# Input transposes of a projection pass: from DMA to TensorE, with the scale and shift applied on the way out

## The reference, cut to what matters

```python
mod = silu(c) @ ada_w + ada_b                       # shift, scale, gate
h   = rms_norm(x, g_pre) * (1 + scale) + shift
u, q, k, v, z = split(h @ w_in)                     # 1024 each, z 2048
y_pool = multiscale_pool(u, pool_w, pool_scale)     # centred means of 2, 4, 8, 16 rows, minus the row
y_ret  = bidir_retention(rope(q), rope(k), v)       # forward and backward chunk scans, per-head norm
out = (concat(y_pool, y_ret) * silu(z)) @ w_out
y   = x + gate * rms_norm(out, g_post)
```

## Time and profile before

| | |
|---|---|
| median of the timed runs | 3350.31 us (3 runs, 3343.3 to 3356.82) |
| the profiled execution's own time | 3349.93 us |
| its span on the slowest core (6) | 3348.4 us |
| spans of the other cores | 3319.5 (core 1) to 3335.5 us (core 3); core 0 3327.2 us |
| granted TensorE clock, mean of a core | 0.976 (core 6) to 0.983 |
| TensorE busy | 3059.1 us (91%) |
| VectorE busy | 2503.0 us (75%) |
| ScalarE busy | 1259.8 us (38%) |
| GpSimd busy | 1233.1 us (37%) |

### The profile page before, as it was taken

How to read it: one execution, slowest core, us unless ns; L and a number is a source line. 1 busy time by engine, 2 the same in 40 slices (tenths; PEclk the granted TensorE clock), 3 DMA queues, 4 the chain that set the end, 5 groups by cost and what they waited for, 6 DMA issues and landing times.

```text
span 3348.4 us, 59437 instructions; the slowest of 8 cores (3319.5 to 3348.4 us)
## 1 busy us (share of the span) xinstructions
PE 3059.1 (91%) x17521; PEld 1551.3 (46%) x17824; DVE 2503.0 (75%) x4781; ACT 1259.8 (38%) x2162; POOL 1233.1 (37%) x1193
## 2 busy tenths in 40 slices
PE   1787778888899999999999999999999999999996
PEld 0343334433345555555555555555555555555553
DVE  1677877757687778877877877887877787787784
ACT  2587555655543223222322323222322222222321
POOL 1233323323333434434444434343433443443433
PEclk9899899999999999999999999999999999999998
DMA  9999999899965555555555555555555555555552
GB/s 185 206 252 243 234 226 242 238 219 241 239 214 127 130 135 140 140 136 138 132 138 137 142 133 141 138 130 137 143 134 139 140 128 140 132 145 130 140 131 73
DMA packets 727915, 542.97 MB, mean 162 GB/s; under 512 B 536112, under 2 KB 592432, under 8 KB 727600
## 3 DMA queue, kind: packets, MB, share of 16 engines
q1 hardware_dynamic: 676848, 453.15, 55.3%
q10 hardware_dynamic: 27648, 62.93, 7.3%
q0 software_dynamic: 23104, 23.07, 5.1%
HBM read 275.28 MB, written 158.86 MB: 130 GB/s over the span
## 4 chain that ended last, share of the span: by engine, by line
PE 70%; DMA 12%; ACT 5%; issue 5%; DVE 4%; POOL 2%; SPq 1%; another core or an unknown queue 1%; ACTq 1%; DVEq 0%; POOLq 0%
PE psum L772 42%; PE psum L1098 20%; PE psum L1027 4%; DMA t_hTg_105<-t_xn_102 3%; DMA t_hTg_107<-t_xn_102 2%; DMA t_hTg_106<-t_xn_102 2%; DMA t_hTg_104<-t_xn_102 1%; DMA ada_sb<-ada_w 1%; SPq L186 1%; POOL t_o_155 L1048 1%; PE psum L995 1%; ACT t_xn_102 L791 1%; PE psum L1008 1%; PE psum L1078 1%; PE psum L1079 1%
## 5 line engine op out<-in xcount | busy, mean ns | idle before, releaser
L1098 PE MATMUL psum<-t_wout,t_yT_158 128*128 128x512 bf16 x3036 | 679.9, 380 | 19.8 <-DMA t_yT_158<-t_yb_157 16.8
L1098 PEld LDWEIGHTS psum<-t_wout,t_yT_158 128*128 128x128 bf16 x3072 | 300.9, 98 | 383.3 <-issue 24.7
L772 PE MATMUL psum<-t_wqz,t_hT_125 128*128 128x512 bf16 x1503 | 344.6, 379 | 1.7
L772 PE MATMUL psum<-t_wqz,t_hT_126 128*128 128x512 bf16 x1473 | 339.0, 379 | 3.3
L772 PE MATMUL psum<-t_wqz,t_hT_127 128*128 128x512 bf16 x1475 | 334.0, 379 | 3.7 <-DVE t_fin_159 L1108 0.4
L957 POOL TENSOR_TENSOR t_kf_150<-t_krB_144,t_kdf 128x1024 bf16<-128x1024 bf16 x94 | 190.6, 2028 | 344.8 <-PE psum L1008 331.8
L998 DVE TENSOR_TENSOR t_scm_151<-psum,t_dtot 128x512 bf16<-128x512 f32 x192 | 125.5, 681 | 256.2 <-PE psum L995 247.6
L1101 ACT ACTIVATE t_fin_159<-psum 128x512 f32<-128x512 f32 x192 | 114.7, 597 | 537.2 <-PE psum L1098 534.1
L1110 POOL TENSOR_TENSOR t_xr_160<-t_xr_160,t_fin_159 128x1024 f32<-128x1024 f32 x96 | 235.7, 2455 | 168.6 <-DVE t_fin_159 L1108 168.6
L772 PEld LDWEIGHTS psum<-t_wqz,t_hT_127 128*128 128x128 bf16 x1536 | 148.8, 98 | 173.5 <-issue 0.5
L772 PEld LDWEIGHTS psum<-t_wqz,t_hT_125 128*128 128x128 bf16 x1536 | 149.0, 98 | 167.3
(11 more groups left out here) (228 smaller groups left out, 6151.0 us busy)
## 6 DMA issues: line engine op xcount, KB each, us to landing
t_xr_160<-x SPq DMA_DIRECT2D x96, 512.0 KB, 3.7
y<-t_xr_160 SPq DMA_DIRECT2D x96, 512.0 KB, 2.7
t_xin_101<-x ACTq DMA_DIRECT2D x48, 512.0 KB, 7.2
t_xin_100<-x ACTq DMA_DIRECT2D x48, 512.0 KB, 8.2
t_krB_144<-krscr SPq DMA_DIRECT2D x96, 256.0 KB, 2.8
vscr<-t_vA_118 SPq DMA_DIRECT2D x48, 256.0 KB, 7.0
krscr<-t_krA_116 SPq DMA_DIRECT2D x48, 256.0 KB, 6.5
vscr<-t_vA_119 SPq DMA_DIRECT2D x48, 256.0 KB, 6.8
```

The lines of the kernel that those rows point to most:

```text
L772: last = e.matmul(bank.ap(), hts(dc), W_[:, dc, col:col + 512], start=(dc == 0), stop=(dc == 7))
L1098: last = e.matmul(pb.ap(), yT[0][:, ec, :], wout[:, ec, sl], start=(ec == 0), stop=(ec == 15))
```

## The change

The DMA transposes of pass A's front go. For each group TensorE now transposes `xn` against an identity matrix (`ident`, made once), 16 blocks of 128x128 in two operations of eight, each operation into one PSUM bank seen as bf16. The scale and shift, until now in place in `hTg`, reads the bank and writes `hTg`: the four feature blocks of the first bank on ScalarE, those of the second on VectorE. `xin` and `ssq` get three buffers (NX), used in turn, `xn` one for each chunk of a group, and `hTg` three (NH), so the front is called one group ahead. The planner learns a cost for a transpose. Apart from that the row loads of `gate_tables` and `pool_tables` (and the loads of pool_w beside them) now wait for the last TensorE operation listed before them, as the weight loads do.

```diff
@@ -60,6 +60,9 @@
 def _est_cost(eng, calls):
     t = 0.0
     for name, a, k in calls:
+        if name == "transpose":
+            t += 0.003 + 0.000417 * 128
+            continue
         if name == "matmul":
             rhs = a[2] if len(a) > 2 else k["rhs"]
             t += 0.003 + 0.000417 * max(_free(rhs), 64)
@@ -320,7 +323,8 @@
 
 GRP = 4
 FG = 2
-NH = 4
+NH = 3
+NX = 3
 NBANKS = 8
 WARM = False
 WARM_GAP = 0.5
@@ -388,6 +392,7 @@
     aft = P([128, 8, 128], BF16, "aft")
     abt = P([128, 8, 128], BF16, "abt")
     bands = P([128, 16, 128], BF16, "bands")
+    ident = P([128, 128], BF16, "ident")
     kdf = P([128, 8], F32, "kdf")
     kdb = P([128, 8], F32, "kdb")
     gcf = P([128, 8], F32, "gcf")
@@ -514,6 +519,8 @@
     ac(lambda e: e.activation(out=scT[:, :, :], in_=cT[:, :, :], func=AF.Silu), [bf("cT")], [sc_b])
 
     dv(lambda e: e.tensor_single_scalar(out=identf[:, :], in_=diff[:, :], scalar=0.0, op=ALU.is_equal), ["diff"], ["identf"])
+    id_b = bf("ident")
+    dv(lambda e: e.tensor_copy(out=ident[:, :], in_=identf[:, :]), ["identf"], [id_b])
     dv(lambda e: e.tensor_single_scalar(out=mge[:, :], in_=diff[:, :], scalar=0.0, op=ALU.is_ge), ["diff"], ["mge"])
     dv(lambda e: e.tensor_single_scalar(out=mlt[:, :], in_=diff[:, :], scalar=0.0, op=ALU.is_lt), ["diff"], ["mlt"])
     dv(lambda e: e.tensor_scalar_max(out=rpos[:, :], in0=diff[:, :], scalar1=0.0), ["diff"], ["rpos"])
@@ -635,9 +642,10 @@
     wout_v = w_out.ap().rearrange("(ec p) n -> p ec n", p=128)
 
     def gate_tables():
-        dma("sp", gpostb[:, :], norm_post.ap().partition_broadcast(128).rearrange("p o n -> p (o n)"), w=[bf("gpostb")])
+        after = [sch.last["pe"]]
+        dma("sp", gpostb[:, :], norm_post.ap().partition_broadcast(128).rearrange("p o n -> p (o n)"), w=[bf("gpostb")], after=after)
         for s in range(nseq):
-            dma("sp", ggt[s][:, :], ada_bg.ap().partition_broadcast(128).rearrange("p o n -> p (o n)"), w=[gg_b[s]])
+            dma("sp", ggt[s][:, :], ada_bg.ap().partition_broadcast(128).rearrange("p o n -> p (o n)"), w=[gg_b[s]], after=after)
             for half in range(2):
                 pg = Bank()
 
@@ -671,10 +679,11 @@
         return paced(go)
 
     def pool_tables():
-        dma("sp", psc_row[:, :], pool_scale.ap().partition_broadcast(128).rearrange("p o n -> p (o n)"), w=[pr_b])
+        after = [sch.last["pe"]]
+        dma("sp", psc_row[:, :], pool_scale.ap().partition_broadcast(128).rearrange("p o n -> p (o n)"), w=[pr_b], after=after)
         pool_v = pool_w.ap().rearrange("g (cc p) d -> p (g cc) d", p=128)
         for hf in range(2):
-            dma("sp", pst[:, :, :], pool_v[:, hf * 4:(hf + 1) * 4, :], w=[ps_b])
+            dma("sp", pst[:, :, :], pool_v[:, hf * 4:(hf + 1) * 4, :], w=[ps_b], after=after)
             dv(lambda e, hf=hf: e.tensor_tensor(out=poolw[:, hf * 4:(hf + 1) * 4, :].rearrange("p (g c) d -> p g c d", g=2),
                                                 in0=pst[:, :, :].rearrange("p (g c) d -> p g c d", g=2),
                                                 in1=psc_row[:, hf * 512:(hf + 1) * 512].rearrange("p (g d) -> p g d", g=2).unsqueeze(2).to_broadcast([128, 2, 2, 256]),
@@ -721,10 +730,10 @@
         return ring(A, *a, log=a_bufs, **k)
 
     a_bufs.append((arena, wv_hi, wk_b + wv_b))
-    xin, xin_b = aring(2, [128, 1024], F32, "xin")
+    xin, xin_b = aring(NX, [128, 1024], F32, "xin")
     xn, xn_b = aring(2, [128, 1024], BF16, "xn")
-    hTg, hTg_b = aring(NH, [128, FG, 8, 128], BF16, "hTg", nb=FG + 8)
-    ssq, ssq_b = aring(2, [128, 4], F32, "ssq")
+    hTg, hTg_b = aring(NH, [128, FG, 8, 128], BF16, "hTg", nb=8)
+    ssq, ssq_b = aring(NX, [128, 4], F32, "ssq")
     rtA, rtA_b = aring(2, [128, 256], F32, "rtA")
     t1A, t1A_b = aring(2, [128, 512], F32, "t1A")
     t2A, t2A_b = aring(2, [128, 512], F32, "t2A")
@@ -775,32 +784,47 @@
 
     na = [0]
 
+    nx = [0]
+
     def a_front(s, g):
         gi = na[0] % NH
         na[0] += 1
         hb = hTg_b[gi]
-        Sched.inherit(hb[:FG], hb[FG:])
         for ci in range(FG - 1, -1, -1):
             c = g * FG + ci
-            sl = (nseq * 1000 - c) % 2
+            sl = nx[0] % NX
+            nx[0] += 1
             dma("act", xin[sl][:, :], xs[s].ap()[c * 128:(c + 1) * 128, :], w=xin_b[sl])
-            op("act", lambda e, sl=sl: e.activation(out=xn[sl][:, :], in_=xin[sl][:, :], func=AF.Square, accum_out=ssq[sl][:, 0:1]),
-               r=xin_b[sl], w=ssq_b[sl] + xn_b[sl])
+            op("act", lambda e, sl=sl, ci=ci: e.activation(out=xn[ci][:, :], in_=xin[sl][:, :], func=AF.Square, accum_out=ssq[sl][:, 0:1]),
+               r=xin_b[sl], w=ssq_b[sl] + xn_b[ci])
             op("pool", lambda e, sl=sl: e.tensor_scalar_add(out=ssq[sl][:, 1:2], in0=ssq[sl][:, 0:1], scalar1=float(D) * EPS), r=ssq_b[sl], w=ssq_b[sl])
             op("pool", lambda e, sl=sl: e.tensor_tensor(out=ssq[sl][:, 2:3], in0=ssq[sl][:, 1:2], in1=mhalf[:, 0:1], op=ALU.pow), r=ssq_b[sl] + [mh_b], w=ssq_b[sl])
-            op("act", lambda e, sl=sl: e.activation(out=xn[sl][:, :], in_=xin[sl][:, :], func=AF.Copy, scale=ssq[sl][:, 2:3]),
-               r=xin_b[sl] + ssq_b[sl], w=xn_b[sl])
-            dma_t("sp", hTg[gi][:, ci, :, :], xn[sl][:, :], r=xn_b[sl], w=[hb[ci]], key=hb[ci])
-        for dc in range(8):
-            v_ = hTg[gi][:, :, dc, :]
-            if dc % 2 == 0:
-                op("dve", lambda e, v_=v_, dc=dc: e.tensor_scalar(out=v_, in0=v_, scalar1=gprime[:, dc, s:s + 1], scalar2=shiftT[:, dc, s:s + 1],
-                                                                  op0=ALU.mult, op1=ALU.add), r=hb[:FG] + [gp_b], w=[hb[FG + dc]])
-            else:
-                op("act", lambda e, v_=v_, dc=dc: e.activation(out=v_, in_=v_, func=AF.Identity, scale=gprime[:, dc, s:s + 1], bias=shiftT[:, dc, s:s + 1]),
-                   r=hb[:FG] + [gp_b], w=[hb[FG + dc]])
+            op("act", lambda e, sl=sl, ci=ci: e.activation(out=xn[ci][:, :], in_=xin[sl][:, :], func=AF.Copy, scale=ssq[sl][:, 2:3]),
+               r=xin_b[sl] + ssq_b[sl], w=xn_b[ci])
+        for hf in range(2):
+            pt = Bank()
+            ptv = lambda pt=pt: pt.ap().bitcast(BF16).rearrange("p (dc t) -> p dc t", dc=4)
+
+            def tr(e, hf=hf, ptv=ptv):
+                last = None
+                for ci in range(FG):
+                    for d4 in range(4):
+                        dc = hf * 4 + d4
+                        last = e.transpose(ptv()[:, d4, ci * 128:(ci + 1) * 128], xn[ci][:, dc * 128:(dc + 1) * 128], ident[:, :])
+                return last
+            op("pe", tr, r=[x for b_ in xn_b for x in b_] + [id_b], w=[pt.b])
+            for d4 in range(4):
+                dc = hf * 4 + d4
+                dst = hTg[gi][:, :, dc, :]
+                src = lambda ptv=ptv, d4=d4: ptv()[:, d4, :].rearrange("p (c t) -> p c t", c=FG)
+                if hf == 1:
+                    op("dve", lambda e, dst=dst, src=src, dc=dc: e.tensor_scalar(out=dst, in0=src(), scalar1=gprime[:, dc, s:s + 1], scalar2=shiftT[:, dc, s:s + 1],
+                                                                                op0=ALU.mult, op1=ALU.add), r=[pt.b, gp_b], w=[hb[dc]])
+                else:
+                    op("act", lambda e, dst=dst, src=src, dc=dc: e.activation(out=dst, in_=src(), func=AF.Identity, scale=gprime[:, dc, s:s + 1],
+                                                                             bias=shiftT[:, dc, s:s + 1]), r=[pt.b, gp_b], w=[hb[dc]])
         dma("sp", rows("h", s, g * FG, FG).rearrange("(c p) n -> p c n", p=128), hTg[gi][:, :, :, :].rearrange("p c a t -> p c (a t)"),
-            r=hb[FG:], w=[scr_b[("h", s, g * FG + ci)] for ci in range(FG)], key=hb[FG])
+            r=hb, w=[scr_b[("h", s, g * FG + ci)] for ci in range(FG)], key=hb[0])
         return gi
 
     nA = [0]
@@ -811,7 +835,7 @@
         r3 = nA[0] % 2
         nA[0] += 1
         ci = c % FG
-        hb = hTg_b[gi][FG:]
+        hb = hTg_b[gi]
         hts = lambda dc: hTg[gi][:, ci, dc, :]
         dma("act", rtA[r3][:, :], ropescr.ap()[c * 128:(c + 1) * 128, :], r=[rsb[c // GRP]], w=rtA_b[r3])
         pv = [Bank(), Bank()]
```

## The result

The changed kernel takes 3250.81 us (median; lowest 3245.67) beside 3351.98 us for the kernel before: a ratio of 0.9696, with an interval of 0.9668 to 0.9724. The forecast was 3260 us. Some executions of any of these kernels are disturbed (the cores of one die run longer at a lower granted clock); ratios leave these out, and where an experiment had too few others, its undisturbed cores are compared. The profiled execution took 3250.5 us; its slowest core is core 2 with a span of 3249.0 us.

What follows compares the result with a forecast made beforehand. Pass A was taken as bound by the arrival of transposed input. Stretch savings of 84.5 us, plus 12 for the prologue, less 6 for row loads, gave 90.5 off 3350.3: 3260 us; range 3200 to 3340.

Steps and rivals of the forecast that it cites:

- So pass A is bound by the arrival of transposed input: Pass A, the first 996 us: TensorE waits for DMA transposes into hTg, which hold 27.6% of the chain of waits.
- The stores behind the transposes: SP's queue in pass A: stores of kr, v and b go out sooner once 96 transposes leave; credited nothing.
- The DMA rival: Pass A: DMA engines stay the bound after the transposes leave, 3293 to 3317, say 3305 us; chance 0.16.
- The rate in the tail: After pass A's inputs: 196 GB/s at DMA share 0.61, some 320 at 1, held against DMA staying the bound.
- Transposes on TensorE, 0.45 us a chunk: Pass A: eight 128x128 transposes a chunk at 0.056 us each, so TensorE needs 7.80 us a chunk.
- the fourth case: Pass A: TensorE stands at its transposes, 2.8 us at each of 47 groups, 132 us, time 3392; chance 0.09.
- VectorE 0.38 for 0.28 us an evacuation: Scale and shift reading PSUM: 0.38 us each on VectorE, 0.2 us a chunk more; ScalarE no change.
- Prologue -12 us: Before the first chunk: 2.1 MB less to load at 175 GB/s, 12 us earlier; bounds 0 and 15.
- 100 to 200 us, -13 and +6 for the rows: 9.7 chunks: TensorE's 82.6 us of work at 95% busy takes 87, saving 13; waits for tied row loads cost 6.
- 200 to 300 us, ScalarE full, -5.5: 10.4 chunks: ScalarE stays at 89.8 us with rope and decay tables; at 95% busy 94.5, saving 5.5.
- 300 to 450 us, -19: 13.7 chunks: VectorE, with band tables, has 124.5 us of work; at 95% busy 131, saving 19.
- 450 to 950 us, TensorE at 95%, -47: 54.3 chunks: TensorE has 431 us of work; at 95% busy 453, saving 47.

Runs made afterwards that it cites:

- the first experiment: Changed kernel with 96 idle DMA transposes put back, one a chunk into an unread spare tile, and two xin buffers: 0.996 of before.
- the control: Changed kernel with two xin buffers in place of three, without any idle transposes: 0.9713 of before.
- the idle copies of 256 B: Changed kernel, two xin buffers, plus an idle plain 256 KB copy a chunk in 1024 runs of 256 bytes: no ratio, lowest time 3244.41 us.
- the tables spread: Changed kernel with set-up tables spread over more chunks and loads for pass B moved later: 0.9628 of before, about 3226 us.
- the early rows: Changed kernel with set-up work spread, plus gate row loads tied to chunk 4 and pool row loads to chunk 55: 0.9636 of before.
- four transposes of 128x128 a chunk: Changed kernel, two xin buffers, plus four idle 128x128 DMA transposes a chunk: 0.9848 of before.

## Why the prediction came out right, and what was wrong in it

The time was right, and the signature it named came: pass B at 896 us for 905 and 2352 us long, clock 0.98 to 0.99, DMA share under 1, transposes 56 ns apart. One sign did not come: 200 to 300 us was to be hardly shorter. By its steps:

- *"So pass A is bound by the arrival of transposed input"*: this step failed. The chain showed where waits ended, and those were the transposes; but with the wait gone and the load left, they end at the stores, and the time is within 0.4% of that before. What held pass A was what the transposes do to the other transfers: 2.9 us a chunk of all the DMA engines, and SP's queue held. The share of 1.03 to 1.12 in the earlier trace rows said the first.
- *The stores behind the transposes, "for which I credit nothing, as TensorE waits for none of them directly"*: this is where the load was left out. VectorE and ScalarE wait for them, 76 us in 400 in the first experiment, since kr and v have two buffers each; GpSimd's scaled k comes after kr, and TensorE stands 24 us behind that (4 in the control). The number held all the same, because the change takes away wait and load together; as to the mechanism, that is luck.
- *The DMA rival* had the right premise (the engines were full) and the wrong price. Its bounds were 1.05 and 2.74 us for a transpose, and I worked out its time from the low end; measured, it is 2.9, a little outside the bounds. (The 2.74 counts every packet under 512 B as a transpose's; by 1056 packets each it would be 2.66.) At the high end its own floor, 366 us for the last stretch, lies under TensorE's time, and the case turns into the forecast. The rate in the tail, which I held against it, told right: the share fell to 0.80.

  The Trainium skill, "DMA: Bandwidth & Descriptors", Specifications, with its 512 B for full rate, pointed to the dear end, and the price agrees. But the idle copies of 256 B cost less than half of it, 1.3 us, so packet size is not all of it here.

- *Transposes on TensorE, 0.45 us a chunk*: right, twice over (0.89 us for sixteen, 1.79 for 32).

  The 275 ns of the Trainium skill, "TensorE: Matmul & The Clock Gate", Part 4, was rightly not used as a price: TensorE's group of L813 has a mean of 223 ns for an instruction (the row is shown at the fourth case), at starts 56 ns apart. Of its second statement, that a transpose does not hold the clock up as a matmul does, nothing shows here: the clock is granted at 0.99 from 450 us on, with 0.9 us of transposes in every 16 us of matmuls.

- *VectorE 0.38 for 0.28 us an evacuation*: 0.34 (1.37/4). ScalarE 0.48, a little cheaper than before.
- *Prologue -12 us*: -11.4 measured, -10.2 by the cores' median, of which 6 came with the ties (4.0 are left without them); the rest is the transposes that left and whatever else the change moves there, which no run takes apart.
- *100 to 200 us, -13 and +6 for the rows*: +4.6 measured, +6.4 by the medians. The 6 was of the right size: TensorE stands 6.8 us behind VectorE's work on the first gg row. What failed is the 95%. On core 2 these eight chunks are 8 x 7.80 + 32 x 0.216 = 69.3 us of work by the prediction's prices; TensorE was busy for 76.2 of 89.6 us at a mean clock of 0.90, as before (0.90), so the sum left out the clock as well as idle time. With the tables spread the stretch takes 80.6 us by the medians for 84.7, but 85.1 with the early rows added; whether the bunching of the set-up work matters in this stretch is not shown.
- *200 to 300 us, ScalarE full, -5.5*: -14.3, by the medians -9.3. ScalarE is as full as I said (88.8%), but it has less to do, 85.4 us from the 11th chunk to the 22nd for 90.6, and it is busy for 94% of that stretch where it was for 87%. Part of this is activation tables: a load, 1283 ns, stands where its work goes to a decay table or a rotary table (lines 540 to 543, 567 and 570 before; none stands at its other lines), and the new order has fewer of them: 19 in these chunks before, 13 after. Before first (185 to 290 us), then after (181 to 270, the same 13 as from the 11th chunk on); x is the count:

```profile
...
L542 ACT ACT_TABLE_LOAD x6 | 7.7, 1283 | 0.1
L567 ACT ACT_TABLE_LOAD x5 | 6.4, 1283 | 1.1 <-DVE t_rred L564 0.9 <-issue 0.2
L570 ACT ACT_TABLE_LOAD x4 | 5.1, 1283 | 0.1
L543 ACT ACT_TABLE_LOAD x3 | 3.8, 1283 | 0.1
L540 ACT ACT_TABLE_LOAD x1 | 1.3, 1283 | 0.3 <-ACT t_vA_119 L824 0.3
...
```

```profile
...
L574 ACT ACT_TABLE_LOAD x5 | 6.4, 1283 | 0.7 <-DVE t_B_124 L881 0.6
L549 ACT ACT_TABLE_LOAD x4 | 5.1, 1283 | 0.1
L547 ACT ACT_TABLE_LOAD x2 | 2.6, 1283 | 0.0
L577 ACT ACT_TABLE_LOAD x1 | 1.3, 1283 | 0.0
L550 ACT ACT_TABLE_LOAD x1 | 1.3, 1283 | 0.0
...
```

  That is 7.7 us less, and other work makes the difference to 5.2. (From 50 to 900 us there are 24 before and 21 after: half of the six fall elsewhere.)
- *300 to 450 us, -19*: -19.5, but -30.9 by the medians; core 6 had been quick there (142.1 us, median 152.6).
- *450 to 950 us, TensorE at 95%, -47*: -46.1 by the medians, 445.5 us for 55 chunks or 8.1 each for 8.2 forecast. The -61.4 of the slowest cores is larger because core 6 was slow there before (509.8 us, median 491.6).
- *The fourth case*, TensorE standing at its transposes: from 50 to 900 us TensorE was idle for 5.2 us in front of them, where the case had 2.8 us in each of 47 groups. It showed twice, for 3.5 us once between 89 and 179 us and for 1.7 us in the prologue, there as the case had it: GpSimd held by a load of gate weights that waits for TensorE, ScalarE by GpSimd's ssq. The row of the transposes (half of them), and two lines of the waits from 50 to 880 us:

```profile
...
L813 PE MATMUL psum<-t_ident,t_xn_104 128*128 128x128 bf16 x376 | 37.3, 223 | 5.2 <-ACT t_xn_104 L802 5.2
...
```

```profile
...
POOL ada_sb L184 <- PE psum L781: 62.7, 2, 55.3
...
ACT t_xn_104 L802 <- POOL t_ssq_109 L801: 16.9, 2, 16.6
...
```

By the medians the terms were missed by +13 us in one stretch and by -4 and -12 in two others: that the total is closer than its parts is in part luck.

What stays open: how the cost divides between the DMA engines and SP's queue; why a packet of a 128x1024 transpose takes the engines twice as long as a plain one of its size (37.5 ns for 19.3; with four transposes of 128x128 a chunk it is 24.5 ns, so transposing alone is not the answer); by which path the ties alone gain 21 us in the kernel before.
